# Mamba-2 stage of a hybrid decoder step: gate z computed with features on partitions, y turned before gating and norm

## What is computed

```
(z, xs, bm, cm, ...) = split(h @ w_in)            # h: 1032 tokens x 1024
xbc = silu(causal_conv(xs, bm, cm))
y   = ssd_scan(xs, dt, A, B, C)  +  d_skip * xs     # 8 chunks of 128 tokens, state carried over them
y   = y * silu(z)
yg  = y.reshape(tokens, 4 groups, 512)
yg  = yg * rsqrt(mean(yg * yg over the 512) + eps)
y   = yg * norm_g                                  # then y @ w_proj_ssm, further on
```

## Time and profile before

| | us |
|---|---|
| median of 3 runs | 3293.85 (3292.9 to 3297.7) |
| profiled execution, its own time | 3297.92 |
| its span, first to last instruction | 3296.1 |
| PE busy | 2974.2 (90%) |
| PE weight loads busy | 2395.6 (73%) |
| DVE busy | 1727.2 (52%) |
| ACT busy | 740.8 (22%) |
| POOL busy | 696.9 (21%) |
| mean granted TensorE clock | 0.931 |

### The profile page before, as it was taken

One profiled execution on the slowest core, in us unless ns is written; L12 is line 12 of the kernel. 1 busy time (PEld: TensorE's weight loads), 2 busy tenths in 40 slices (PEclk: granted clock), 3 DMA queues, 4 the chain that ended last, 5 costly groups with the idle time before them and its releaser, 6 DMA issues. The chain is left out here.

```text
span 3296.1 us, 39605 instructions
## 1 busy us (share of the span) xinstructions
PE 2974.2 (90%) x15815; PEld 2395.6 (73%) x15815; DVE 1727.2 (52%) x2881; ACT 740.8 (22%) x1543; POOL 696.9 (21%) x422
## 2 busy tenths in 40 slices
PE   6999999988996588999999984999879999999997
PEld 3888555556884375676675753999869898988986
DVE  1323799995552256646537454245543535445355
ACT  4121211106773013414324233000031000000001
POOL 0000121104210112122222233233212323232220
PEclk7999999997996589999999987999989999999999
DMA  6110233320003031130121105232231111111111
GB/s 191 37 65 26 86 118 118 107 73 2 1 2 106 24 107 45 42 85 23 47 77 39 42 23 165 77 131 95 86 129 52 39 52 39 52 39 52 39 39 52
DMA packets 212181, 216.13 MB, mean 66 GB/s; under 512 B 15282, under 2 KB 191418, under 8 KB 211931
## 3 DMA queue, kind: packets, MB, share of 16 engines
q1 hardware_dynamic: 188302, 164.64, 16.1%
q10 hardware_dynamic: 20096, 37.14, 3.2%
q0 software_dynamic: 3600, 11.82, 1.1%
HBM read 167.60 MB, written 46.10 MB: 65 GB/s over the span
## 5 line engine op out<-in xcount | busy, mean ns | idle before, releaser
L2026 PE MATMUL ps<-h_lo,w_hi 128*128 128x344 f32 x1056 | 338.7, 321 | 3.9 <-PEq L2238 3.9
L2028 PE MATMUL ps<-h_hi,w_lo 128*128 128x344 f32 x1056 | 338.1, 320 | 0.0
L2027 PE MATMUL ps<-h_hi,w_hi 128*128 128x344 f32 x1056 | 338.0, 320 | 0.0
L2008 POOL CAST w_hi<-w_raw 128x2048 fp32r<-128x2048 f32 (+1 forms) x50 | 97.2, 1945 | 902.6 <-PE ps L2028 803.5
L1488 PE MATMUL ps<-hT,ring 128*128 128x344 f32 x864 | 262.8, 460 | 0.0
L1567 PE MATMUL ps<-ring,hT 128*128 128x256 f32 x1024 | 236.0, 392 | 7.8 <-PEq L1144 6.8
L452 PE MATMUL ps<-ring,hT 128*128 128x256 f32 (+3 forms) x1152 | 238.4, 369 | 1.0 <-PEq L213 1.0
L2010 POOL TENSOR_TENSOR w_lo<-w_raw,w_hi 128x2048 fp32r<-128x2048 f32 (+1 forms) x50 | 233.7, 4674 | 4.0
L1567 PEld LDWEIGHTS ps<-ring,hT 128*128 128x128 f32 x1024 | 201.2, 198 | 42.8 <-issue 11.9
L1488 PEld LDWEIGHTS ps<-hT,ring 128*128 128x128 f32 x864 | 166.0, 194 | 90.8 <-issue 15.8
L597 PE MATMUL ps<-hT,ring 128*128 128x344 f32 x768 | 225.8, 455 | 1.3 <-DMA ring<-in_w_in 1.3
(11 more groups left out here) (385 smaller groups left out, 5756.1 us busy)
## 6 DMA issues: line engine op xcount, KB each, us to landing
ring<-in_w_in SPq DMA_DIRECT2D x31, 1024.0 KB, 5.5
ring<-in_w_ada SPq DMA_DIRECT2D x24, 1024.0 KB, 6.2
w_raw<-in_w_ffn_in SPq DMA_DIRECT2D x44, 512.0 KB, 5.0
w_raw<-in_w_ffn_out SPq DMA_DIRECT2D x10, 1024.0 KB, 5.0
s_sig<-sig ACTq DMA_DIRECT2D x16, 516.0 KB, 5.0
m_sig<-s_sig ACTq DMA_DIRECT2D x16, 516.0 KB, 3.3
stt<-in_state_ssm SPq DMA_DIRECT2D x32, 256.0 KB, 3.4
out_ssm_sample<-stt SPq DMA_DIRECT2D x32, 256.0 KB, 4.7
```

The lines of the kernel that those rows point to most:

```text
L2008: self.nc.gpsimd.tensor_copy(hi, raw).then_inc(self.hi_done, 1)
L2026: nc.tensor.matmul(out, ah, bl, start=(i == 0), stop=False)
L2027: nc.tensor.matmul(out, ah, bh, start=False, stop=False)
L2028: mm = nc.tensor.matmul(out, al, bh, start=False, stop=(i == len(terms) - 1))
```

## The change

`z` is computed with features on partitions: 128 weight columns stationary, 344 columns of `hT` moving, of which the last 8 are the samples. This makes 12 units of 8 matmuls a group in place of 16 and the 32 sample matmuls. The gate and the norm then run on turned y: `turn` takes y as it is, DVE gates it out of PSUM into `yT` (512 columns), ACT squares it, POOL adds the two halves of the squares (256 columns), and PE sums them over partitions with two matmuls by a matrix of ones (`sum_squares`), which leaves each token's sum on all partitions, 128x128. Mean, root and reciprocal are 128x128, and a multiplication of 128x512 scales y. These steps run one or two chunks late, in an order of their own. In `front` the C*B and turned-B matmuls go behind the segment sums, and wait for the mean of the chunk three before, since they share bank 0.

```diff
@@ PE
-                tr(ps[:, 0, P:2 * P], post[:, 4, cols], K.ident[:])
-                mm(ps[:, 0, 0:P], post[:, 4, cols], post[:, 5, cols], start=True, stop=True).then_inc(bcb_ps, 1)
...
                 s.then_inc(seg_ps, 1)
+                if n:
+                    pe.wait_ge(cb_done, 2 * n)
+                if g and c == 0:
+                    pe.wait_ge(ymean, n)
+                if c >= 3:
+                    pe.wait_ge(ymean, n - 2)
+                tr(ps[:, 0, P:2 * P], post[:, 4, cols], K.ident[:])
+                mm(ps[:, 0, 0:P], post[:, 4, cols], post[:, 5, cols], start=True, stop=True).then_inc(bcb_ps, 1)
...
             def turn(g, c):
                 n = TT * g + c
-                pe.wait_ge(ynormed, n + 1)
+                pe.wait_ge(*((y_ready, n - g) if c else (yd_done, 2 * (n + 1))))
                 pe.wait_ge(cb_done, 2 * min(n + 3, TT * (g + 1)))
-                if c == TT - 1:
-                    pe.wait_ge(yT_done, n)
+                if c >= TT - 2:
+                    pe.wait_ge(ymean, n)
...
+            def sum_squares(g, c):
+                pe.wait_ge(yfolded, TT * g + c + 1)
+                for j in range(2):
+                    a = mm(ps[:, 0, 0:P], K.ones[:], ysq2[:, P * j:P * j + P], start=(j == 0), stop=(j == 1))
+                a.then_inc(ysum_ps, 1)
...
             def z_unit(g, u):
...
-                    a = mm(ps[:, 1 + u % 2, 0:256], hT[:, k, P * t:P * t + P], w[:, k, :], start=(k == 0), stop=(k == KB - 1))
+                    a = mm(ps[:, 1 + u % 2, 0:CW], w[:, k, P * (f % 2):P * (f % 2) + P],
+                           hT[:, k, CW * c:CW * c + CW], start=(k == 0), stop=(k == KB - 1))
                 a.then_inc(z_ps, 1)
-
-            def z_samples(g, i):
...
-                raw_at, spread_at = (1, 4) if g else (10, 13)
-                for u in range(2 * TT):
+                raw_at, spread_at = (1, 3) if g else (8, 10)
+                for u in range(ZU):
...
                         unit(g + 1, before[c + 1] - 1)
+                    if c:
+                        sum_squares(g, c - 1)
             turn(GROUPS - 1, TT - 1)
+            sum_squares(GROUPS - 1, TT - 1)
@@ POOL
+            def fold(g, c):
+                n = TT * g + c
+                pool.wait_ge(ysquared, n + 1)
+                v.tensor_tensor(ysq2[:, 0:2 * P], ysq2[:, 0:2 * P], ysq2[:, 2 * P:4 * P], ALU.add).then_inc(yfolded, 1)
@@ ACT, chunk loop
                 for c in range(TT):
+                    if c >= 2:
+                        root(g, c - 2)
                     if c + 1 < TT:
                         decay(g, c + 1)
...
                     for j in units[:-1]:
                         keep(g + 1, j)
+                    if c >= 2:
+                        out(g, c - 2)
                     if c:
-                        out(g, c - 1)
+                        square(g, c - 1)
                     for j in units[-1:]:
                         keep(g + 1, j)
-                    norm(g, c)
@@ DVE, chunk loop
                 for c in range(TT):
+                    if c >= 2:
+                        mean(c - 2)
                     if c + 1 < TT:
                         front(c + 1)
                     back(c)
-                    scale(c)
+                    if c >= 2:
+                        divide(c - 2)
+                    if c:
+                        gate(c - 1)
                     if g + 1 < GROUPS:
                         for f in blocks_at[c]:
                             convolve(g + 1, f)
+                mean(TT - 2)
+                divide(TT - 2)
+                gate(TT - 1)
+                mean(TT - 1)
+                divide(TT - 1)
```

More of the change, by code:

```diff
@@ L1339, in ssm @@
         block = ctx.enter_context(nc.Block())
+        ZU = 4 * TC
         here = [3, 3, 2, 2, 2, 2, 2, 2]
@@ L1465, in _ @@
                     if c >= 2:
-                        store(g, c - 2)
+                        fold(g, c - 2)
+                    if c >= 3:
+                        store(g, c - 3)
+                fold(g, TT - 2)
+                store(g, TT - 3)
+                fold(g, TT - 1)
                 store(g, TT - 2)
@@ L1611, in _ @@
             for g in range(GROUPS):
-                raw_at, spread_at = (1, 4) if g else (10, 13)
-                for u in range(2 * TT):
+                raw_at, spread_at = (1, 3) if g else (8, 10)
+                for u in range(ZU):
                     z_unit(g, u)
-                    if u == 0 and g:
+                    if g and u == 0:
                         turn(g - 1, TT - 1)
                         final_state(g - 1)
+                    if g and u == 1:
+                        sum_squares(g - 1, TT - 1)
                     if u == raw_at:
@@ L1621, in _ @@
                         spread(g, 0)
-                    if g and u == 12:
+                    if g and u == 9:
                         spread(g, 1)
-                    if u % TT == TT - 1:
-                        z_samples(g, u // TT)
                 if g == 0:
@@ L1680, in decay, with square @@
                              ACT.Exp).then_inc(m_exp, 1)
-            def norm(g, c):
+            def square(g, c):
                 n = TT * g + c
@@ L1708, in _ @@
             for g in range(GROUPS):
-                for u in range(2 * TT):
-                    i, t = u // TT, u % TT
-                    act.wait_ge(z_ps, 2 * TT * g + u + 1)
+                for u in range(ZU):
+                    f, c = u // TC, u % TC
                     if g and u == 0:
-                        act.wait_ge(ygated, TT * g)
-                    a.activation(z[:, t, 256 * i:256 * i + 256], ps[:, 1 + u % 2, 0:256], ACT.Silu).then_inc(z_done, 1)
+                        root(g - 1, TT - 2)
+                        out(g - 1, TT - 2)
+                        square(g - 1, TT - 1)
+                    act.wait_ge(z_ps, ZU * g + u + 1)
+                    a.activation(zT[:, f, CW * c:CW * c + CW], ps[:, 1 + u % 2, 0:CW], ACT.Silu).then_inc(z_done, 1)
                     if u == 0 and g:
+                        keep_final(g - 1)
+                    if u == 1 and g:
+                        root(g - 1, TT - 1)
                         out(g - 1, TT - 1)
-                        keep_final(g - 1)
                     if g == 0 and u in first_silu:
                         silu(0, first_silu.index(u))
-                    if u == (1 if g else 10):
+                    if u == (1 if g else 8):
                         act.wait_ge(rows_ps, g + 1)
@@ L1751, in _ @@
                         silu(g + 1, f)
+            root(GROUPS - 1, TT - 2)
+            out(GROUPS - 1, TT - 2)
+            square(GROUPS - 1, TT - 1)
+            root(GROUPS - 1, TT - 1)
             out(GROUPS - 1, TT - 1)
@@ L1911, in back, with gate, mean, divide @@
                         v.tensor_tensor(state[:], state[:], ps[:, 3, :], ALU.add).then_inc(s_done, 1)
-                    i = c % 2
-                    dve.wait_ge(ysquared, n + 1)
-                    v.tensor_scalar(stat[:, 1, i:i + 1], stat[:, 0, i:i + 1], 1.0 / GW, EPS, ALU.mult, ALU.add).then_inc(ymean, 1)
-                def scale(c):
+                def gate(c):
                     n = TT * g + c
-                    i = c % 2
+                    dve.wait_ge(yT_ps, n + 1)
+                    if n >= 2:
+                        dve.wait_ge(yT_out[c % 2], 16 * (n // 2))
+                    v.tensor_tensor(yT[:, c % 2], ps[:, 0, :].rearrange("p (k n) -> p k n", k=4), zT[:, :, P * c:P * c + P],
+                                    ALU.mult).then_inc(ygated, 1)
+                def mean(c):
+                    n = TT * g + c
+                    dve.wait_ge(ysum_ps, n + 1)
+                    if n >= 2:
+                        dve.wait_ge(ynormed, n - 1)
+                    v.tensor_scalar(spreads[:, c % 2, :], ps[:, 0, 0:P], 1.0 / GW, EPS, ALU.mult, ALU.add).then_inc(ymean, 1)
+                def divide(c):
+                    n = TT * g + c
                     dve.wait_ge(yroot2, n + 1)
-                    link(v.reciprocal(stat[:, 3, i:i + 1], stat[:, 2, i:i + 1]), ystep, ny)
-                    v.tensor_scalar(y[:, i, :], y[:, i, :], stat[:, 3, i:i + 1], None, ALU.mult).then_inc(ynormed, 1)
+                    v.reciprocal(spreads[:, c % 2, :], spreads[:, c % 2, :]).then_inc(yinv, 1)
+                    dve.wait_ge(yinv, n + 1)
+                    v.tensor_tensor(yT[:, c % 2], yT[:, c % 2], spreads[:, c % 2, :].unsqueeze(1).to_broadcast([P, 4, P]),
+                                    ALU.mult).then_inc(ynormed, 1)
                 front(0)
                 for c in range(TT):
+                    if c >= 2:
+                        mean(c - 2)
                     if c + 1 < TT:
```

69 lines of the change are left out of this document (26 added, 43 removed).

## The result

The changed kernel takes 3331.93 us (median of 4 runs, 3329.01 to 3334.36); the kernel before, on the same chip, 3295.77 (4 runs, 3292.9 to 3298.22). The ratio is 1.0115, with a 95% interval of 1.0099 to 1.0131: **slower by 1.2%**, about 36 us. The profiled execution took 3329.01, with a span of 3327.2 us and a mean granted clock of 0.933; beside the profiled one of before it is 31.1 us longer.

What follows compares the result with a forecast made beforehand. The prediction took PE, busy 90% of the span, and its waits as the bound. Terms -23.3 - 2.5 + 19.3 + 35.8 = +29.3 us on the 3293.85 us median gave 3323 us, range 3300 to 3345.

Steps and rivals of the forecast that it cites:

- z stages of groups 1 to 3: Sample matmuls and the slow clock behind them go; 64.7 us instead of 72.9 to the samples' sum; -23.3 us together.
- z stage of group 0: Stage ends with DVE, so PE's saving counts only by bringing `spread(0, 0)` forward: -2.5 us.
- chunk stages of groups 0 to 2: New waits for fold and mean outweigh the nine xdt waits that go: +19.3 us over three groups.
- last group: No units as cover: 16.3 us a chunk instead of 11.93, and a serial end; +35.8 us, between +28 and +45.
- the +0.5 at each start: Start of each middle group's chunk stage: xdt(0) comes later behind the segment sums, +0.5 us a group.
- the sums' waits: Middle chunk stages: PE waits 1.4 us before `sum_squares`, from chunk 2 on, for division, scaling, squares and fold.
- The waits for the mean: `front` of middle chunks: C*B waits for DVE's mean behind its convolution, by 0.6, 2.3 and 3.3 us.
- Fold and reciprocal: Links of the norm's chain: POOL's fold of 256 columns taken as 0.6 us, DVE's 128x128 reciprocal as 0.95 us.
- The bound of +45: Upper end for the last group's cost, if `back` too ran at the half clock.
- The covered waits: Rival: middle groups' new waits overlap away, stages 6 us shorter instead of 19 longer; 3298 us, chance 0.10.
- the norm off PE's path everywhere: Rival: the norm's chain never delays PE, even in the last group, which ends faster; -34, 3260 us, chance 0.05.
- The fallen clock: Rival: clock falls behind new waits in middle stages, a third of 24 chunks losing 2.5 us; +20, 3343 us, chance 0.15.

Runs made afterwards that it cites:

- Experiment 3: Kernel before, without the 32 sample matmuls a group and their Silu, samples' y gated with other values: 3259.48 us, ratio 0.9888.
- Experiments 1: Changed kernel with DVE's gate ahead of the older chunk's division and ACT's squares ahead of scaling: 3308.93 us, ratio 1.0034 to the kernel before.
- 2: Changed kernel with DVE taking the mean right behind the gate, ahead of the convolution: 3311.86 us, ratio 1.0042 to the kernel before.
- 5: Changed kernel with gate and squares ahead of division and scaling, and the mean ahead of the convolution: 3275.17 us, ratio 0.9935 to the kernel before.
- version 4: Changed kernel with C*B and turned B, with their waits, back ahead of the segment sums in `front`: 3372.72 us, ratio 1.0225 to the kernel before.
- Version 6: As 5, but squares summed in bank 4, one chunk later behind `front`, with mean, root and group-end steps moved: 3262.92 us, ratio 0.9907 to before.
- version 9: The same kernel as Version 6, timed again in another set: 3263.36 us, ratio 0.9898 to the kernel before.

## Why the prediction was right, and where its sizes were off

The forecast was 3323 us, slower, within 3300 to 3345; measured were 3332. Direction and mechanism held: the waits stand on the lines it named, and the time is in the stages it named. The medians lie 36.2 us apart and the profiled executions 31.1. The ledger explains the 31.1; the other 5 us are the spread of the executions, since the profiled one was above the median before the change and below it after. By the prediction's steps:

| step | predicted | measured |
|---|---|---|
| z stages of groups 1 to 3 | -23.3 | -21.2 (-6.7, -8.0, -6.6) |
| z stage of group 0 | -2.5 | -3.0, and +0.5 in its start |
| chunk stages of groups 0 to 2 | +19.3 | +24.7 |
| last group | +35.8 | +33.5 |
| after the block | 0 | -3.4 |
| sum | +29.3 | +31.1 |

That the sums agree to 2 us is partly luck: the chunk stages cost 5.4 us more and the z stages gave 2.1 less, while the last group cost 2.3 less and 3.4 came off behind the block, where nothing was predicted and no cause is known.

- **z stages.** Right. The sample matmuls took the slow clock with them, and the samples' sum waits: 3.37 us in group 1 (2 were predicted) and 2.08 in the other two. Experiment 3 gives the size of the whole item, 8.7 to 9.6 us a stage. The distance that the prediction gives as 14.3 us, from 1453.09 to 1467.64, is 14.55; the 11.2 that it takes from it is right.
- **Chunk stages.** From the third `front` on 132.1 us in each group, where 129.8 were worked out, and nothing of the +0.5 at each start. The stage has six of the sums' waits, 8.1 us in the records; the seventh, 0.93 us, stands in the z head, where 1.0 was predicted. PE, when it waits, also loses the overlap with the unit before (its record is 4.79 us long, and the next start comes after 4.63), so from start to start the six cost 9.1 us, against 8.4 by six of 1.4. The waits for the mean are 5.25 us in the records (3.11 and 2.13, in chunks 2 and 5 as it said) and 5.6 from start to start; the prediction had 6.2, in three of 0.6, 2.3 and 3.3. Behind a wait the sum itself takes 0.54 us to the next start and not 0.44, 0.6 us a group. The term that was too small is the clock behind the waits, priced at nothing in the forecast and kept for a rival: the unit of 6.48 us in place of 4.79 is 1.7 us a group. Together (+0.7, -0.6, +0.6, +1.7) this is the whole difference of 2.3. Experiments 1, 2 and 5 show the two waits to be the causes: with both edits the three periods lose 47.2 us, more than the 36.6 us of waits that went (42.8 less the 6.2 left in the z heads).
- **Fold and reciprocal.** The fold takes 0.72 us in 26 of 32 chunks, 1.39 in six and 0.845 in the mean, where 0.6 was taken. The six long folds are the ones ahead of the sums' waits of 1.79 us; in the middle groups the other sums wait 1.13 us or less. The reciprocal of 128x128 takes 947 ns, as the two rows of before gave (0.95).
```profile
L1950 DVE RECIPROCAL ssm_rms<-ssm_rms 128x128 f32<-128x128 f32 x32 | 30.3, 947 | 15.5 <-ACT ssm_rms L1705 15.5
```

- **Last group.** Three sizes were off, and cancel in part. The four chunks from the fourth `front` on take 63.3 us, 15.8 each, not 16.3: the segment sums were put wholly at the half clock, and took 2.81 to 3.62 us, 2.81 in the chunk shown. From the mask's end to the next sum the prediction had 7.6 us, and the row has 7.5. Chunk 6 costs +6.3 in place of +8.2, and the first ones -0.9 in place of +2. The end costs +12.5 in place of +7.8: after a wait of 5.83 us the back part of chunk 7 ran at the half clock, 3.51 + 2.02 + 1.91 us, about twice what such matmuls take a chunk earlier (1.90, 1.08, 1.02). The bound of +45 had allowed for that; the number had not.
- **Rivals.** The covered waits and the norm off PE's path everywhere are excluded by the 70.2 us of waits on L1574. The fallen clock is there behind one wait a group in the middle (of 3.11, 3.12 and 2.13 us), some 5 us of the 20 it was given. But version 4, with waits of 5.27, 4.29 and 1.98 us, shows it in full: 15 us more of busy time.
- The change's own gain is real. The changed kernel's z stages show 24 us of it; experiment 3 would put it at up to 37, the last group's 5.4 us of clock included. The changed kernel gives back 58 us in the chunk stages and the last group, by the order of steps around the norm: 5 and 6 keep every matmul and are 57 and 69 us faster. 5 differs from it in the order on DVE and ACT alone, 6 also in the bank and in where PE's sum stands.

## What to carry to other kernels

When a reduction moves to partitions and becomes a chain over four engines, count what stands ahead of each of its links on every queue, and let the link that others wait for (gate, squares, mean) go before those that nobody waits for yet (division, scaling). A PSUM bank that the chain shares with the next chunk's first matmuls ties PE to it. Version 6, with another bank, one chunk of delay and the moves of mean and root that go with them, is 12 us faster than 5; what each of these gave was not measured apart. The last pass of a loop has no cover: predict it by itself.

## What was not expected of the hardware

- A mask of DVE with two SBUF operands did not end earlier for starting earlier beside a product of POOL: it ended 1.07 to 1.11 us after it, in the kernel before as well. Its 1.97 us in the late chunks of before, and 3.25 in version 9, look like work; with POOL idle it takes 1.21 to 1.23.
- A wait costs more than its length where the clock falls behind it: version 4 added 21.8 us of waits and 37.0 us of time in the three periods, in one execution each. In the changed kernel the chunk stage of group 1, with six waits of 1.1 to 1.8 us, two for the mean and one slow unit, is at 0.98. The length of the wait just before does not decide it alone: one of 3.12 us in group 2 was followed by a unit of 4.79 us, one of 2.13 by a unit of 6.48.
